# Second block's layer norms: the mean is spread a second time, kept in SBUF, and GpSimd subtracts it from the last chunks

## The chip, the cores and the metric

The kernel runs on one core of one Trainium2 chip. The metric is the device time of the whole program in microseconds. A time per run and, for one profiled execution, a hardware trace are at hand. TensorE is called PE (its weight loads PEld), VectorE DVE, ScalarE ACT, GpSimd POOL, and SyncE SP.

## The reference

Two transformer-like blocks run one after the other on one sequence of 512 tokens and 1024 features, all in float32. The first block is an SSM and sliding-window attention mixer followed by a gated FFN, with RMS norms. The second block has two layers, called "a" (dilated attention) and "h" (HGRN2). Each layer has two deep-norm residual steps:

```
x = layer_norm(ALPHA * x + mixer(x), ln_mix_g[i], ln_mix_b[i])
x = layer_norm(ALPHA * x + squared_relu_mlp(x), ln_ffn_g[i], ln_ffn_b[i])

def layer_norm(x, g, b):
    mu = mean(x, axis=-1);  var = mean(square(x - mu), axis=-1)
    return (x - mu) * rsqrt(var + 1e-5) * g + b
```

So the second block has four layer norms: `mix_a`, `ffn_a`, `mix_h`, `ffn_h`. The text calls them the first, second, third and fourth norm. They lie at about 1265, 1627, 1886 and 2250 us of the trace. The result of the fourth is the output of the kernel.

## The kernel before

Activations are held feature-major: a tensor of 1024 features by 512 tokens is eight chunks (`DC` = 8), each 128 partitions (features) by 512 columns (tokens). Every dense product is done in three matmuls of rounded parts: `w_lo*x_hi`, `w_hi*x_lo`, `w_hi*x_hi`. ACT makes the rounded high part (`w_hi`, `x_hi`) with a copy that rounds; DVE makes the low part as the difference (`w_lo = raw - w_hi`, `x_lo = h - x_hi`), with both inputs in SBUF. Weights come in slabs of 128 x 2048 by SP's DMA queue into two slots.

Each engine has its own program with explicit semaphores; the order within an engine is the order written. `settle` is DVE's drain.

How a layer norm goes. PE sums the chunks over features token by token with matmuls of one column (`token_sum`, L687). DVE makes the mean by token (`mean4`, 128 x 4, L2450) and the variance (L2455), ACT its root (L1601), DVE the reciprocal (`rstd4`, L2459). PE spreads both over 128 partitions with four transposes each (`spread`, L694): the mean into PSUM bank 4 (`SPREAD_MEAN`), then the reciprocal root into bank 5. Then DVE goes through the chunks (`layer_norm`, L2461 on): it subtracts the mean from chunks 0 and 1 (L2462), and for each chunk c multiplies by the reciprocal root (L2466, "mul c" in the text) and then subtracts the mean from chunk c+2 (L2468, "sub c+2"). Both instructions read one operand from SBUF (`y`) and one from PSUM.

In the first three norms more work of DVE lies in the same loop, because the next stage of matmuls starts on the chunks as they are finished. For chunks 0 and 1 DVE also makes `h` (gain and bias, a TENSOR_SCALAR from SBUF to SBUF, L2471) and `x_lo` (L1731). After `x_lo` of chunk 1 it makes the low part of the second weight slab (`second_lo`, L1717, two halves; one half before `hgrn_in`, in the second norm). From chunk 2 on, ACT makes `h` (L1609) and then `x_hi` (L1611) of each chunk, and DVE makes `x_lo` of chunk c-1 after mul c. In the fourth norm (`after` is `None`) ACT makes `h` of every chunk, and SP sends it out.

PE's next stage is `first_pair` (first and third norm, L617, L622, L627) or `first_triple` (second norm, L1219, L1224, L1229). It goes by a written order of (weight slab, chunk) steps; for `first_pair` it is `(0,0), (0,1), (1,0), (1,1), (0,2), (0,3), (0,4), (1,2), ...`, each step six matmuls. A step waits for `x_hi` of its chunk before its first two matmuls and for `x_lo` before its last two; step (1,0) waits for `w_lo` of the second slab before its middle two. For `first_triple` the order is `(0,0), (0,1), (1,0), (0,2), ...`, and a step of slab 1 has three matmuls.

POOL is used in the first block for `accumulate` (L522 and L525, two-operand instructions on 128 x 512 chunks in SBUF) and then only to issue small DMAs in the attention (`send`, the last at 1183 us). In the four layer norms it does nothing.

The buffer `root` (128 x 512, SBUF) holds the shift used in the variance sums of the norm (ACT writes it, L1593; DVE reads it, L2394, L2396, L2422); it is free while the loop of L2461 on runs. PSUM bank 6 (`MEAN`) holds the sums by token until DVE has read them at L2450.

Of the kernel before, what the change touches and what calls it, by code (L numbers as in the profile page):

```python
# [18 lines left out]
DC = D // P  # L19
# [76 lines left out]
def build(nc, w, x_in, gains_in, lam_in, sink_in, bc_in, c_in, pos_in, iota_in, const_in, freq_in, mask_in, rope2_in,  # L96
          hmask_in, out):
    f32, f32r, bf16, i32 = mybir.dt.float32, mybir.dt.float32r, mybir.dt.bfloat16, mybir.dt.int32
    ALU, ACT, AX = mybir.AluOpType, mybir.ActivationFunctionType, mybir.AxisListType
# [33 lines left out]
    y = at("y", Y_AT, [DC, T])  # L133
# [76 lines left out]
    root = extra("root", [T])  # L210
# [49 lines left out]
    ps = nc.alloc_psum_tensor("ps", [P, 8, T], f32)  # L260
# [44 lines left out]
    def sem(name):  # L305
        return nc.alloc_semaphore(name)
# [20 lines left out]
    folded = sem("folded")  # L327
    var4_ready = sem("var4_ready")
    mean_ready = sem("mean_ready")
    root_ready = sem("root_ready")  # L330
    result_ready = sem("result_ready")
    rstd_ready = sem("rstd_ready")
# [79 lines left out]
    LO_SPLITS1 = {1: 0, 6: 1, 8: 2, 13: 3}  # L412
    GLUS1 = {8: 1, 11: 2, 14: 3}
    NEAR2 = [min(b, 1) + 1 for b in range(TB)]

    def shift_at(st):

# [51 lines left out]
    with nc.Block() as block:  # L469
# [40 lines left out]
        @block.gpsimd  # L510
        def _(pool):
            for pads in (ab_re, ab_neg, ca_re, ca_im):
                last = pool.memset(pads[:, :, :, :], 0.0)
            last.then_inc(pads_zero, 1)
            pool.wait_ge(mask_ready, 1)
            pool.memset(k_tau[:, :, :, :], 0.0).then_inc(kt_zero, 1)

            def accumulate(name, event):

                for c in range(DC - 1):  # L520
                    pool.wait_ge(y_ready, YB[event] + c + 1)
                    last = pool.tensor_tensor(acc_sq if c else acc, y[:, c, :], y[:, c, :], ALU.mult)  # L522
                    if c:
                        pool.drain()
                        last = pool.tensor_tensor(acc, acc, acc_sq, ALU.add)  # L525
                    if c < DC - 2:
                        pool.drain()
                last.then_inc(acc_ready, 1)

            def send(pa, old):  # L530

                pool.wait_ge(o2_ready, TB * pa + TB)
                if not (isinstance(pa, int) and pa == 0):
                    pool.wait_ge(joined, pa)
                pool.sem_inc(sums_sent, 1)
                for hh in range(2):
                    for b in range(TB):
                        pool.dma_start(o_far[:, hh, b, :], o_class[32 * b:32 * b + 32, old, hh, :, :]).then_inc(far_ready, 16)

            for name, event in ACCS[:2]:  # L540
                accumulate(name, event)
            send(0, 0)
            with pool.Fori(0, HEAD_PAIRS // 2 - 1) as i:
                send(2 * i + 1, 1)
                send(2 * i + 2, 0)

        @block.tensor
        def _(pe):
# [148 lines left out]
            def spread_rstd(name):  # L697
                pe.wait_ge(rstd_ready, SK_ROOT[name] + 1)
                spread(SPREAD[name], rstd4).then_inc(rstd_spread, 1)
# [365 lines left out]
            def dense_normed(name, part, layer, xs=None, hid=None, operand=None, begun=0):  # L1065
# [42 lines left out]
                pe.wait_ge(mean4_ready, nth + 1)  # L1108
                spread(SPREAD_MEAN, mean4).then_inc(mean_spread, 1)
                spread_rstd(var)  # L1110

            def norm_and_ffn(layer, proj, up, down):

# [135 lines left out]
        def _(act):  # L1249
# [352 lines left out]

            def normed(layer, part, n, after):

                for c in range(DC):
                    act.wait_ge(y_ready, YB[f"res_{part}_{layer}"] + c + 1)
                    g, b = gain(f"ln_{part}_g{n}", c), gain(f"ln_{part}_b{n}", c)
                    if c > 1 or not after:
                        last = act.activation(h[:, c, :], y[:, c, :], ACT.Identity, scale=g, bias=b)  # L1609
                    if after:  # L1610
                        act.activation(x_hi[:, c, :], y[:, c, :], ACT.Identity, scale=g, bias=b).then_inc(xhi_ready, 1)  # L1611
                    else:
                        last.then_inc(result_ready, 1)

            def norm_and_ffn(layer, proj, up, down, n, after):
                normed_out(proj, layer, "mix")
# [82 lines left out]
        def _(dve):  # L1699
# [746 lines left out]
            def layer_norm(layer, part, n, after):  # L2446
# [16 lines left out]
                settle()  # L2463
                dve.wait_ge(rstd_spread, NTH_SPREAD[var] + 1)
                for c in range(DC):
                    tt(y[:, c, :], y[:, c, :], scale, ALU.mult).then_inc(y_ready, 1)  # L2466
                    if c + 2 < DC:
                        tt(y[:, c + 2, :], y[:, c + 2, :], mean, ALU.subtract)  # L2468
                    if after and c < 2:
                        settle()  # L2470
                        ts(h[:, c, :], y[:, c, :], gain(f"ln_{part}_g{n}", c), gain(f"ln_{part}_b{n}", c), ALU.mult, ALU.add)  # L2471
                        settle()
                        part_lo(after, c, h[:, c, :])
                        if c:
                            for half in range(1 if after == "hgrn_in" else 2):
                                second_lo("hgrn_in" if after == "hgrn_in" else after + "0", half)
                    elif after and c > 2:
                        part_lo(after, c - 1, h[:, c - 1, :])
                    if c + 2 < DC:
                        settle()  # L2480
# [244 lines left out]
```

## Time and profile before

| what | value |
|---|---|
| time before, median of 3 runs | 2270.08 us |
| lowest and highest | 2269.61 and 2271.3 us |
| span of the profiled execution (first to last instruction) | 2267.5 us |
| own time of the profiled execution | not recorded; 2.6 us more than its span if it was a median run |
| PE busy | 2165.4 us (95% of the span) |
| DVE busy | 1271.7 us (56%) |
| ACT busy | 885.9 us (39%) |
| POOL busy | 84.4 us (4%) |
| mean granted TensorE clock | 0.970 |

The page has one execution: the busy time by engine, the span in 40 slices, the DMA queues, the chain of work that ended last, and groups of instructions. Positions below are microseconds from the start of the span. A timeline row has the start, the duration, the engine, the line and the tiles, and in brackets the idle time of the engine before it and what ended it. "PE 1.12 x4" is a merged row of four instructions: the time is from the start of the first to the end of the last. Durations of neighbours on an engine overlap by about 0.1 us.

### The profile page before, as it was taken

How to read it: one execution, taken by the hardware profiler on the slowest of the kernel's cores; microseconds unless marked ns; L12 is line 12 of the kernel's file. 1: busy time of each engine (PE TensorE's matmuls, PEld its weight loads, DVE VectorE, ACT ScalarE, POOL GpSimd, SP SyncE). 2: the span in 40 equal slices, each digit the busy share in tenths (PEclk: the TensorE clock that was granted, in tenths of full speed). 3: DMA queues.
4: the chain of work that ended last, by engine and by line, in shares of the span. 5: the costliest groups of instructions: out<-in, count | busy, mean ns of one | idle time of the engine just before them, and what ended most of it. 6: DMA issues, size and time to landing. Idle time of an engine off the chain costs nothing.

```text
span 2267.5 us, 29414 instructions
## 1 busy us (share of the span) xinstructions
PE 2165.4 (95%) x11002; PEld 1771.0 (78%) x11002; DVE 1271.7 (56%) x2003; ACT 885.9 (39%) x1298; POOL 84.4 (4%) x91
## 2 busy tenths in 40 slices
PE   6979899999999999999999899999999998999997
PEld 5747778888877888888877688888777776888886
DVE  6986464434455566665566742344568877423444
ACT  4224233222227555565553431242254534312322
POOL 1000300000130000000000000000000000000000
PEclk9989999999999999999989899999999998999998
DMA  4001322233232212222221132222212121322221
GB/s 166 30 10 56 112 75 92 84 103 107 73 116 84 89 49 87 72 86 70 84 83 56 56 101 103 93 93 93 75 56 74 56 93 56 104 101 93 93 93 56
DMA packets 32980, 185.48 MB, mean 82 GB/s; under 512 B 5760, under 2 KB 6144, under 8 KB 14208
## 3 DMA queue, kind: packets, MB, share of 16 engines
q1 hardware_dynamic: 27792, 176.31, 22.6%
q10 hardware_dynamic: 3312, 6.14, 0.8%
q0 software_dynamic: 1792, 1.90, 0.3%
q8 instruction: 55, 0.90, 0.2%
q14 instruction: 29, 0.24, 0.0%
HBM read 180.06 MB, written 2.10 MB: 80 GB/s over the span
## 4 chain that ended last, share of the span: by engine, by line
PE 81%; DVE 10%; DVEq 4%; ACT 2%; issue 1%; DMA 1%; ACTq 0%
PE ps L566 12%; PE ps L567 12%; PE ps L568 12%; PE ps L1047 5%; PE ps L1049 5%; PE ps L1048 5%; PE ps L1098 2%; PE ps L1100 2%; PE ps L1099 2%; PE ps L687 1%; PE ps L627 1%; PE ps L617 1%; PE ps L984 1%; PE ps L967 1%; PE ps L980 1%
## 5 line engine op out<-in xcount | busy, mean ns | idle before, releaser
L1268 ACT ACTIVATE w_hi<-raw 128x2048 fp32r<-128x2048 f32 (+1 forms) x122 | 226.1, 1853 | 298.6 <-PE ps L568 220.2
L566 PE MATMUL ps<-x_hi,w_lo 128*128 128x512 f32 x816 | 317.6, 389 | 0.5 <-DVE y L2185 0.3
L568 PE MATMUL ps<-x_hi,w_hi 128*128 128x512 f32 x816 | 317.5, 389 | 0.0
L567 PE MATMUL ps<-x_lo,w_hi 128*128 128x512 f32 x816 | 317.4, 389 | 0.0
L1708 DVE TENSOR_TENSOR w_lo<-raw,w_hi 128x2048 fp32r<-128x2048 f32 (+3 forms) x116 | 259.2, 2235 | 93.9 <-ACT w_hi L1268 93.6
L1047 PE MATMUL ps<-x_hi,w_lo 128*128 128x512 f32 x544 | 218.9, 402 | 2.4 <-DVE w_lo L2337 2.4
L1049 PE MATMUL ps<-x_hi,w_hi 128*128 128x512 f32 x544 | 213.2, 392 | 0.0
L1048 PE MATMUL ps<-x_lo,w_hi 128*128 128x512 f32 x544 | 212.3, 390 | 0.0
L566 PEld LDWEIGHTS ps<-x_hi,w_lo 128*128 128x128 f32 x816 | 153.2, 188 | 33.0 <-issue 0.7
L568 PEld LDWEIGHTS ps<-x_hi,w_hi 128*128 128x128 f32 x816 | 153.2, 188 | 31.9
L567 PEld LDWEIGHTS ps<-x_lo,w_hi 128*128 128x128 f32 x816 | 153.2, 188 | 31.6
L568 PE MATMUL ps<-hid_hi,w_hi 128*128 128x512 f32 x378 | 147.1, 389 | 0.0
L566 PE MATMUL ps<-hid_hi,w_lo 128*128 128x512 f32 x378 | 147.0, 389 | 0.0
L567 PE MATMUL ps<-hid_lo,w_hi 128*128 128x512 f32 x378 | 147.0, 389 | 0.0
L2337 DVE TENSOR_TENSOR w_lo<-raw,w_hi 128x2048 fp32r<-128x2048 f32 x38 | 87.1, 2291 | 76.1 <-ACT w_hi L1481 75.8
L2369 DVE TENSOR_TENSOR tmp<-tmp 128x512 f32<-128x512 f32 x64 | 44.2, 691 | 144.7 <-ACT hid_hi L1560 144.6
L1049 PEld LDWEIGHTS ps<-x_hi,w_hi 128*128 128x128 f32 x544 | 102.5, 188 | 22.6
L1047 PEld LDWEIGHTS ps<-x_hi,w_lo 128*128 128x128 f32 x544 | 102.6, 189 | 21.8 <-DVE w_lo L2337 2.8
L1048 PEld LDWEIGHTS ps<-x_lo,w_hi 128*128 128x128 f32 x544 | 102.9, 189 | 19.7
L1518 ACT ACTIVATE swapped<-ps 32x512 f32<-32x512 f32 x192 | 113.0, 589 | 2.3
L1558 ACT ACTIVATE tmp<-ps 128x512 f32<-128x512 f32 x64 | 38.2, 597 | 178.2 <-PE ps L568 175.3
L1509 ACT ACTIVATE qkv<-ps 128x512 f32<-128x512 f32 x72 | 42.9, 597 | 142.2 <-PE ps L1049 141.9
(452 smaller groups left out, 4050.3 us busy)
## 6 DMA issues: line engine op xcount, KB each, us to landing
raw<-w_attn_in SPq DMA_DIRECT2D x32, 1024.0 KB, 4.9
raw<-w_gate_up SPq DMA_DIRECT2D x22, 1024.0 KB, 4.9
raw<-w_up_a SPq DMA_DIRECT2D x16, 1024.0 KB, 4.8
raw<-w_down_a SPq DMA_DIRECT2D x16, 1024.0 KB, 4.9
raw<-w_up_h SPq DMA_DIRECT2D x16, 1024.0 KB, 4.9
raw<-w_down_h SPq DMA_DIRECT2D x16, 1024.0 KB, 4.9
raw<-w_hgrn_in SPq DMA_DIRECT2D x8, 1024.0 KB, 4.8
raw<-w_down SPq DMA_DIRECT2D x8, 768.0 KB, 4.3
```

The source lines that it names most:

```text
L566: pe.matmul(o, w_lo[:, slot, a:a + P], hi[:, k, :], start=k == 0, stop=False)
L567: pe.matmul(o, w_hi[:, slot, a:a + P], lo[:, k, :], start=False, stop=False)
L568: last = pe.matmul(o, w_hi[:, slot, a:a + P], hi[:, k, :], start=False, stop=k == st.kc - 1)
L1047: pe.matmul(o, w_lo[:, slot, a:a + P], x_hi[:, k, :], start=k == 0, stop=False)
L1048: pe.matmul(o, w_hi[:, slot, a:a + P], x_lo[:, k, :], start=False, stop=False)
L1049: last = pe.matmul(o, w_hi[:, slot, a:a + P], x_hi[:, k, :], start=False, stop=k == DC - 1)
L1098: pe.matmul(o, w_lo[:, slot, a:a + P], hi[:, k, :], start=k == 0, stop=False, skip_group_check=True)
L1099: pe.matmul(o, w_hi[:, slot, a:a + P], lo[:, k, :], start=False, stop=False, skip_group_check=True)
L1268: act.activation(w_hi[:, slot, 0:width], raw[:, slot, 0:width], ACT.Copy).then_inc(whi_ready, 1)
L1518: last = act.activation(turned[to:to + 32], bank[at_:at_ + 32], ACT.Copy)
L1708: tt(w_lo[:, slot, 0:width], raw[:, slot, 0:width], w_hi[:, slot, 0:width].bitcast(f32), ALU.subtract) \
L2337: tt(w_lo[:, n0 % 2, :], raw[:, n0 % 2, :], w_hi[:, n0 % 2, :].bitcast(f32), ALU.subtract) \
```

## The change

- PE: after the reciprocal root is spread, the mean is spread once more, into bank 6 (`MEAN`), and signalled by `mean_again`.
- ACT: `keep_mean` waits for that and copies bank 6 to `root` in SBUF, signalled by `mean_kept`. In the first three norms the copy stands after `x_hi` of chunk 0; in the fourth it stands before the first chunk.
- POOL: at the end of its program it waits in each norm for `mean_kept` and subtracts `root` from chunks 4 to 7 (in the fourth norm 5 to 7) of `y` in place, each signalled by `centred`.
- DVE: it leaves out L2468 for these chunks and waits for `centred` before it multiplies them.

```diff
--- before.py
+++ after.py
@@ -327,6 +327,7 @@
     folded = sem("folded")
     var4_ready = sem("var4_ready")
     mean_ready = sem("mean_ready")
+    mean_again, mean_kept, centred = sem("mean_again"), sem("mean_kept"), sem("centred")
     root_ready = sem("root_ready")
     result_ready = sem("result_ready")
     rstd_ready = sem("rstd_ready")
@@ -412,6 +413,8 @@
     LO_SPLITS1 = {1: 0, 6: 1, 8: 2, 13: 3}
     GLUS1 = {8: 1, 11: 2, 14: 3}
     NEAR2 = [min(b, 1) + 1 for b in range(TB)]
+    ON_POOL = [(4, 5, 6, 7)] * 3 + [(5, 6, 7)]
+    CENTRED = [0, 4, 8, 12]
 
     def shift_at(st):
 
@@ -543,6 +546,10 @@
             with pool.Fori(0, HEAD_PAIRS // 2 - 1) as i:
                 send(2 * i + 1, 1)
                 send(2 * i + 2, 0)
+            for nth in range(len(MEANS)):
+                pool.wait_ge(mean_kept, nth + 1)
+                for c in ON_POOL[nth]:
+                    pool.tensor_tensor(y[:, c, :], y[:, c, :], root[:, :], ALU.subtract).then_inc(centred, 1)
 
         @block.tensor
         def _(pe):
@@ -1108,6 +1115,7 @@
                 pe.wait_ge(mean4_ready, nth + 1)
                 spread(SPREAD_MEAN, mean4).then_inc(mean_spread, 1)
                 spread_rstd(var)
+                spread(MEAN, mean4).then_inc(mean_again, 1)
 
             def norm_and_ffn(layer, proj, up, down):
 
@@ -1602,6 +1610,14 @@
 
             def normed(layer, part, n, after):
 
+                nth = MEANS[f"mean_{part}_{layer}"]
+
+                def keep_mean():
+                    act.wait_ge(mean_again, nth + 1)
+                    act.activation(root[:, :], ps[:, MEAN, :], ACT.Copy).then_inc(mean_kept, 1)
+
+                if not after:
+                    keep_mean()
                 for c in range(DC):
                     act.wait_ge(y_ready, YB[f"res_{part}_{layer}"] + c + 1)
                     g, b = gain(f"ln_{part}_g{n}", c), gain(f"ln_{part}_b{n}", c)
@@ -1611,6 +1627,8 @@
                         act.activation(x_hi[:, c, :], y[:, c, :], ACT.Identity, scale=g, bias=b).then_inc(xhi_ready, 1)
                     else:
                         last.then_inc(result_ready, 1)
+                    if after and c == 0:
+                        keep_mean()
 
             def norm_and_ffn(layer, proj, up, down, n, after):
                 normed_out(proj, layer, "mix")
@@ -2463,8 +2481,10 @@
                 settle()
                 dve.wait_ge(rstd_spread, NTH_SPREAD[var] + 1)
                 for c in range(DC):
+                    if c in ON_POOL[nth]:
+                        dve.wait_ge(centred, CENTRED[nth] + c + 1 - ON_POOL[nth][0])
                     tt(y[:, c, :], y[:, c, :], scale, ALU.mult).then_inc(y_ready, 1)
-                    if c + 2 < DC:
+                    if c + 2 < DC and c + 2 not in ON_POOL[nth]:
                         tt(y[:, c + 2, :], y[:, c + 2, :], mean, ALU.subtract)
                     if after and c < 2:
                         settle()
```

## Rows read from the trace of the kernel before

**Rows 1.** The page: the span, and the chain that ended last by engine.
```profile
span 2267.5 us, 29414 instructions
...
PE 81%; DVE 10%; DVEq 4%; ACT 2%; issue 1%; DMA 1%; ACTq 0%
```

**Rows 2.** Chain, first norm: start us, us, engine, written tile, line.
```profile
1277.28 0.69 DVE y L2466
...
1284.54 0.73 PE ps L627 x2
```

**Rows 3.** Timeline, first norm: start us, us, instruction, [idle before <-releaser].
```profile
1268.28 1.12 PE L694 MATMUL ps<-consts,by_token 128*128 128x128 f32 x4 [0.98 <-DVE by_token L2459]
...
1270.19 0.81 ACT L1611 ACTIVATE x_hi<-y,gains 128x512 fp32r<-128x512 f32 x1 [1.06 <-DVE y L2466]
...
1271.45 0.69 DVE L1731 TENSOR_TENSOR x_lo<-h,x_hi 128x512 fp32r<-128x512 f32 x1
...
1273.60 0.55 DVE L2471 TENSOR_SCALAR h<-y,gains 128x512 f32<-128x512 f32 x1
...
1274.22 0.69 DVE L1731 TENSOR_TENSOR x_lo<-h,x_hi 128x512 fp32r<-128x512 f32 x1
...
1274.83 2.35 DVE L1717 TENSOR_TENSOR w_lo<-raw,w_hi 128x1024 fp32r<-128x1024 f32 x2
...
1277.24 0.74 PE L622 MATMUL ps<-x_hi,w_lo 128*128 128x512 f32 x2 [1.07 <-DVE w_lo L1717]
...
1277.88 0.68 DVE L2468 TENSOR_TENSOR y<-y,ps 128x512 f32<-128x512 f32 x1
...
1282.56 0.73 PE L627 MATMUL ps<-x_lo,w_hi 128*128 128x512 f32 x2 [0.32 <-DVE x_lo L1731]
```

**Rows 4.** Chain, second norm, columns as in rows 2.
```profile
1638.46 0.70 DVE y L2466
...
1640.00 0.71 ACT x_hi L1611
...
1640.75 0.73 PE ps L1219 x2
```

**Rows 5.** Timeline, fourth norm, columns as in rows 3.
```profile
2257.35 0.69 DVE L2466 TENSOR_TENSOR y<-y,ps 128x512 f32<-128x512 f32 x1
...
2262.80 1.28 DVE L2466 TENSOR_TENSOR y<-y,ps 128x512 f32<-128x512 f32 x2
2263.52 1.52 ACT L1609 ACTIVATE h<-y,gains 128x512 f32<-128x512 f32 x2 [0.55 <-DVE y L2466]
```

**Rows 6.** Line L1593: duration ns min/median/max, first and last start us.
```profile
L1593 ACT ACTIVATE root<-ps x4: 598/599/599, 1236.1 to 2174.6; 128x512 f32<-128x512 f32 x4
```

**Rows 7.** Timeline of POOL and DVE in the first block, columns as in rows 3.
```profile
252.70 1.29 POOL L525 TENSOR_TENSOR tmp<-tmp 128x512 f32<-128x512 f32 x1
...
614.50 1.04 POOL L522 TENSOR_TENSOR tmp<-y 128x512 f32<-128x512 f32 x1 [5.77 <-DVEq L2191]
614.89 1.99 DVE L1708 TENSOR_TENSOR w_lo<-raw,w_hi 128x1280 fp32r<-128x1280 f32 x1 [0.52 <-ACT w_hi L1268]
615.68 2.35 POOL L525 TENSOR_TENSOR tmp<-tmp 128x512 f32<-128x512 f32 x1
```

**Rows 8.** Lines L1708 (603 to 650 us) and L2549, columns as in rows 6.
```profile
L1708 DVE TENSOR_TENSOR w_lo<-raw,w_hi x8: 1493/2152/2294, 603.7 to 649.5; 128x1280 fp32r<-128x1280 f32 x4, 128x2048 fp32r<-128x2048 f32 x4
...
L2549 DVE TENSOR_SCALAR state<-state,f_cum x48: 285/286/290, 1675.9 to 1841.2; 128x128 f32<-128x128 f32 x48
L2549 DVE TENSOR_SCALAR state<-ps,f_cum x8: 351/352/353, 1675.1 to 1836.4; 128x128 f32<-128x128 f32 x8
```

**Rows 9.** Windows, first norm: busy us of each engine, granted clock, DMA share.
```profile
1256.00:1257.00 1.00, 0.00 (x0) 0.00 (x0) 0.93 (x3) 0.04 (x1) 0.00 (x0) 1.00 0.00 0
1257.00:1258.00 1.00, 0.28 (x2) 0.31 (x2) 0.52 (x1) 0.00 (x0) 0.00 (x0) 0.64 0.00 0
...
1274.00:1275.00 1.00, 1.00 (x5) 0.74 (x5) 0.93 (x3) 0.00 (x0) 0.00 (x0) 0.83 0.00 0
```

## The prediction

> **What bounds the kernel now.** I read the page first: its chain goes through PE for 81% of the span and through DVE for 10% [rows 1]. In the middle of a matmul stage an instruction taken from DVE is worth nothing; around the layer norms PE stands still or waits for chunks, and there DVE is the chain. So I went through the chain and the timeline around the four norms.
>
> First norm: DVE starts mul 2 at 1277.28, and that is on the chain; the last time PE is behind DVE is the last pair of step (0,4), at 1284.54, which ends at 1285.27 [rows 2]. From there PE is the chain. Before that, PE waits 1.07 us for `w_lo` of the second slab and then only fractions such as 0.32 us for `x_lo` [rows 3]. So what the end of the norm pays for has two halves. The stretch up to mul 2 (DVE makes `h`, `x_lo` of chunks 0 and 1, and `w_lo`) is paid in full. Behind it, the loop over chunks 2 to 4 is paid only as far as PE catches up with it. The third norm has the same rows. In the second, mul 2 at 1638.46 goes through ACT's `x_hi` to PE at 1640.75, and behind this PE is the chain [rows 4]: there, all of the cost of DVE up to mul 2 counts, and nothing after it. In the fourth norm there is no PE work left; DVE's loop and ACT's last `h` are the end of the program [rows 5].
>
> **What the change removes.** It takes four L2468 from the first three norms each, three from the fourth. One is 0.68 us [rows 3], 0.60 from start to start, and all of them stand behind mul 2.
>
> Fourth norm: mul 2 to mul 6 take 2262.80 - 2257.35 = 5.45 us for four chunks, 1.36 each [rows 5]. Mul 3 stays at 2258.71. Without sub 5 to 7 a mul follows the last after 0.69 + 0.07 = 0.76: mul 6 starts at 2261.0 and ends at 2261.7 instead of 2263.5. ACT's last two `h` hang on it as before, 0.71 apart [rows 5]. The output DMA follows each `h`. Gain 1.8 us, all at the end of the program. It needs POOL in time: I put the end of the spread near 2254.9 (mul 0 starts at 2254.63), the copy takes 0.60 [rows 6], so POOL starts at about 2255.6; at 1.29 us for a two-operand instruction of this shape [rows 7] it has finished chunks 5, 6, 7 by 2259.5, and DVE wants them at 2260.2 to 2261.6. All of DVE's instructions here have `y` in SBUF and the other operand in PSUM.
>
> First norm, were POOL free of charge: mul 2 stays, mul 3 to 7 come closer. But ACT makes two instructions per chunk, 0.71 us apart, so chunks can't come faster than 1.42 us, where they come every 1284.54 - 1282.56 = 1.98 now [rows 2, 3] (mul, sub, `x_lo` and a drain). `x_hi` of chunk 2 is then ready at 1277.28 + 0.69 + 0.02 + 0.71 + 0.81 = 1279.5 as now, that of chunk 4 at 1282.5. Step (0,4) of PE, six matmuls in 1.38 us, ends at 1284.2 instead of 1285.27: gain 1.0. Third norm the same, second norm nothing, because PE takes no time from DVE behind mul 2. With the fourth norm: -3.8 us. That is the most the change can give.
>
> **What it adds.** PE: four more transposes, 1.12 us as a row of four at the lower clock [rows 3], while PE would stand idle until `x_hi` of chunk 0; nothing. ACT: one copy, 599 ns [rows 6], after `x_hi` of chunk 0, where ACT has over a microsecond free until mul 1; nothing (0.1 us in the fourth norm, under mul 1). Behind ACT's wait for the spread stand `h` and `x_hi` of later chunks, none due yet. The queues of SP are not touched; POOL has nothing behind its waits.
>
> POOL and DVE together are the disputed cost. In the first block POOL did L525 in 1.29 us when DVE was idle, and in 2.35 us when DVE had begun a `w_lo` before it: it ended 1.15 us after DVE. The other way round, L522 runs from 614.50 to 615.54 and the DVE's L1708 that starts at 614.89 takes 1.99 us [rows 7] where the quickest of this shape takes 1.49 [rows 8]: 0.50 us of waiting, 0.15 less than the overlap. So an instruction of DVE with both operands in SBUF and a two-operand one of POOL do not run together; the later one waits for the whole of the earlier. The page "SBUF — State Buffer" of the Trainium skill, section "Who interferes with whom", says so: DVE with two SBUF inputs and GpSimd reading SBUF exclude one another for a whole instruction. By that rule, the trace agrees.
>
> Does L2471, one operand, SBUF to SBUF, also exclude POOL? L2549 takes 286 ns from SBUF and 352 from PSUM on 128 columns [rows 8], 66 ns less, and 0.55 us on 512 columns against 0.69 for others [rows 3]: the SBUF form is the quicker one, so it may use a second way to SBUF. I take it that it waits. "VectorE: DVE Perf Modes", section "The perf-mode tier table", gives a float32 `tensor_scalar` in SBUF the double rate, with both read ports; by that it would stand in POOL's way too. If it did not, the delay would be some 0.6 us less in each of three norms, and the sum below 4.0 instead of 5.8.
>
> Where does POOL's work fall? First norm: ACT's copy starts at 1270.19 + 0.72 = 1270.9, ends at 1271.5, POOL starts at 1271.6. DVE's `x_lo` of chunk 0 has begun at 1271.45 [rows 3], so sub 4 runs from about 1272.1 to 1273.3 and sub 5 to 1274.5. These are the very microseconds in which DVE has `h` (1273.60), `x_lo` (1274.22) and two halves of `w_lo` (1274.83 to 1277.18), all SBUF [rows 3]. If both take turns, `h` waits 0.9 us for sub 5, `x_lo` 1.2 for sub 6, the first half of `w_lo` 1.2 for sub 7, less three times the 0.15: 2.9 us late at mul 2. If POOL goes through without giving way, `h` waits 3.3: nearly the same. Bounds: below 0 to 0.3 (DVE never gives way and POOL fits in behind), above 3.3. I take 2.9, by the exclusion seen both ways in rows 7.
>
> First norm with 2.9: mul 2 at 1280.2, `x_hi` of chunk 4 at 1285.4 (by ACT's 1.42 and once more DVE), step (0,4) ends at 1286.9: +1.6. Third +1.6. Second norm: the same three waits (one half of `w_lo` only), +2.9 in full. Fourth -1.8. Together +4.3.
>
> The clock: PE is idle through the window at 1256 and most of that at 1257, and within the latter its granted clock falls from 1.00, that is from 2.4 to 1.2 GHz (mean 0.64); it comes back in the window at 1274, where PE has worked for some microseconds [rows 9]. Now PE is to idle 1.07 + 2.9 = 4.0 us before `w_lo` [rows 3], as long as there or longer. If the clock falls for some 3 us of work, these cost 1.5 us more, less what PE waits anyway. Between 0 and 1.4 us for each of three norms; I take 0.5 each, +1.5. Sum +5.8: 2267.5 + 5.8 = 2273.3 of span; the median of the runs shown is 2.6 us above the span, so **2276 us**.
>
> **Rivals.** (A) DVE keeps SBUF through instructions that stand without a drain between them (`x_lo`, both `w_lo`): POOL gets in only at the two drains. Delay 0.75 + 1.05 = 1.8: first and third norm +0.6, second +1.8, fourth -1.8, sum +1.2, and up to 2.5 of clock: 2271 to 2274, say 2272.5. For it: DVE's neighbours overlap. Against: nothing in the rows shows an engine that is passed over when it waits. (B) The other sign: POOL costs DVE next to nothing, at most 0.3 us per norm, because the waiting POOL always loses to DVE's next instruction, or because the long rows of L525 have another cause. It holds if the delay stays under 1.4 us per norm; then -3.5: 2266.5. For it: DVE does not need chunk 4 before about 1280, so POOL may come last without harm. Against it: the 0.50 us that L1708 waited. (C) The delay, and the clock falls in every norm for long, or POOL is slow to begin after its long rest: +4.3 + 4.2 or more, 2279 and above. (D) The delay is absorbed further on, by slack in the next stage: 2270. Against it: PE is the chain there [rows 1].
>
> **Numbers.** Mine 0.42, A 0.22, B 0.25, C 0.07, D 0.04. The measurement can tell about 0.2%, 4.5 us, from no change. Faster by that would need more than the 3.8 us above: 0.04. Mine lies over it nine times in ten (0.38), A seldom (0.06), C always: slower 0.51. Same 0.45. The range reaches from B to the lower end of C: 2266 to 2280; for my case alone 2273 to 2279.5.
>
> **What would show it.** L2471 and L1731 of chunk 1 and L1717 with rows over 1.3 us in the first three norms; L2468 nine times instead of 24; POOL rows of 1.3 to 2.5 us beside them; mul 2 of the first three norms 2 to 3.3 us later after mul 0 than now; PE's clock lower in the stretch behind `w_lo`; the last `h` 1.8 us sooner after mul 0 of the fourth norm. I am wrong if DVE's rows keep their lengths (B), if only one or two of them grow (A), or if POOL's first instruction starts late enough to miss this stretch.

## The result, and the profile after

The changed kernel takes 2275.88 us (median of 8 runs, 2272.62 to 2278.81), the kernel before on the same chip 2270.02 us (8 runs, 2268.45 to 2271.3). The ratio is 1.0027, 95% interval 1.0018 to 1.0037: 5.9 us slower, and the interval excludes 1. In the later runs of the same kernel (`e9` below) it was 1.0024 (1.0014 to 1.0034). The profiled execution has its own time, 2276.1 us, and a span of 2274.3 us, 6.8 more than the span before. In every run whose span is on record the time is 1.7 to 1.9 us above the span, so the profiled execution before took about 2269.3 us, 0.7 less than its median; that is most of the difference between 6.8 and 5.9.

The page of the changed kernel: span, busy time by engine, and the chain by engine.

```profile
span 2274.3 us, 29450 instructions
...
PE 2164.5 (95%) x11018; PEld 1768.4 (78%) x11018; DVE 1271.7 (56%) x1988; ACT 888.1 (39%) x1302; POOL 106.4 (5%) x106
...
PE 83%; DVE 9%; DVEq 4%; ACT 2%; issue 1%; DMA 1%; ACTq 0%
```

DVE's busy time is 1271.7 us, as before, although it has 15 subtractions fewer. Those took 0.60 us each from start to start, 9.0 together; 8.0 of it is back in the three rows per norm that follow. DVE's timeline of the changed kernel in the first norm, from mul 0 to mul 2 (L2486 is mul, L2488 sub, L2491 `h`, L1749 `x_lo`, L1735 `second_lo`):

```profile
1271.36 0.69 DVE L2486 TENSOR_TENSOR y<-y,ps 128x512 f32<-128x512 f32 x1
...
1272.72 0.55 DVE L2491 TENSOR_SCALAR h<-y,gains 128x512 f32<-128x512 f32 x1
1273.34 0.69 DVE L1749 TENSOR_TENSOR x_lo<-h,x_hi 128x512 fp32r<-128x512 f32 x1
1274.13 0.69 DVE L2486 TENSOR_TENSOR y<-y,ps 128x512 f32<-128x512 f32 x1
...
1275.49 1.20 DVE L2491 TENSOR_SCALAR h<-y,gains 128x512 f32<-128x512 f32 x1
1276.77 1.61 DVE L1749 TENSOR_TENSOR x_lo<-h,x_hi 128x512 fp32r<-128x512 f32 x1
1278.30 3.44 DVE L1735 TENSOR_TENSOR w_lo<-raw,w_hi 128x1024 fp32r<-128x1024 f32 x2
1281.83 1.47 DVE L2486 TENSOR_TENSOR y<-y,ps 128x512 f32<-128x512 f32 x2
```

And what POOL does, its timeline in the four norms (one merged row each; in brackets how long it had idled and for what):

```profile
1273.46 6.06 POOL L552 TENSOR_TENSOR y<-y,root 128x512 f32<-128x512 f32 x4 [88.78 <-ACT root L1617]
...
1637.09 6.05 POOL L552 TENSOR_TENSOR y<-y,root 128x512 f32<-128x512 f32 x4 [357.56 <-ACT root L1617]
1901.68 6.05 POOL L552 TENSOR_TENSOR y<-y,root 128x512 f32<-128x512 f32 x4 [258.55 <-ACT root L1617]
2263.78 3.73 POOL L552 TENSOR_TENSOR y<-y,root 128x512 f32<-128x512 f32 x3 [356.05 <-ACT root L1617]
```

The fourth norm shows what one subtraction takes when nothing with both operands in SBUF runs beside it: 3.73 / 3 = 1.24 us. In the first three, four take 6.06, 1.1 us more than 4 x 1.24; one by one their records in the first norm are 1.71, 1.28, 1.46 and 1.73 us long. The same microseconds, 1273.5 to 1279.5, hold DVE's `h`, `x_lo` and first half of `w_lo`, which grew by 0.65, 0.92 and 1.09 us over rows 3 (0.55, 0.69, 2.35). That is 2.66 us, and mul 2 comes 2.7 us later. In DVE's work for chunk 0, before POOL begins, every row is as it was.

How PE pays for it. The chain of the changed kernel in the first norm: start, us, engine, written tile, line.

```profile
1275.49 1.20 DVE h L2491
...
1276.77 1.61 DVE x_lo L1749
1278.38 2.23 DVEq L2500
1280.61 1.15 DVE w_lo L1735
...
1281.80 0.73 PE ps L629 x2
...
1287.19 0.73 PE ps L624 x2
...
1288.39 0.46 PE ps L634 x2
```

The kernel before has mul 0 of this norm here:

```profile
1269.47 0.69 DVE L2466 TENSOR_TENSOR y<-y,ps 128x512 f32<-128x512 f32 x1
```

The lengthened rows are themselves links. PE waits until 1281.80 for `w_lo` of the second slab, and step (0,4) ends at 1288.85, 17.49 us after mul 0, where it was 1285.27 - 1269.47 = 15.80.

In the fourth norm all goes the other way. DVE and ACT of the changed kernel, timeline:

```profile
2267.27 3.62 DVE L2486 TENSOR_TENSOR y<-y,ps 128x512 f32<-128x512 f32 x5
2267.99 3.86 ACT L1625 ACTIVATE h<-y,gains 128x512 f32<-128x512 f32 x5 [0.55 <-DVE y L2486]
```

Five muls now follow one another at 0.73 us, and the last `h` ends 8.67 us after mul 0 (2263.18), where rows 5 give 2265.04 - 2254.63 = 10.41.

The following table is worked out from such rows of both timelines, each stretch from the start of mul 0 of its norm. "PE's end" is the end of step (0,4) in the first and third norm and of the 72 matmuls of `first_triple` in the second.

| stretch | before | after | difference |
|---|---|---|---|
| mul 1 to mul 2, first / second / third | 5.04 / 3.91 / 5.04 | 7.70 / 6.55 / 7.70 | +2.66 / +2.64 / +2.66 |
| mul 0 to PE's end, first | 15.80 | 17.49 | +1.69 |
| mul 0 to PE's end, second | 22.32 | 27.44 | +5.12 |
| mul 0 to PE's end, third | 15.80 | 17.47 | +1.67 |
| mul 0 to the last `h`, fourth | 10.41 | 8.67 | -1.74 |

For the second norm, mul 0 and the last matmul of the 72, before (the first two rows) and after:

```profile
1631.78 0.69 DVE L2466 TENSOR_TENSOR y<-y,ps 128x512 f32<-128x512 f32 x1
1653.71 0.39 PE L1229 MATMUL ps<-x_lo,w_hi 128*128 128x512 f32 x1
...
1634.99 0.69 DVE L2486 TENSOR_TENSOR y<-y,ps 128x512 f32<-128x512 f32 x1
1662.04 0.39 PE L1237 MATMUL ps<-x_lo,w_hi 128*128 128x512 f32 x1
```

It has 2.5 us above its wait of 2.64. Windows of the changed kernel there: us of the window, then busy us of PE, PEld, DVE, ACT and POOL, granted clock, DMA share, GB/s.

```profile
1641.00:1642.00 1.00, 0.00 (x0) 0.00 (x0) 1.00 (x2) 0.00 (x0) 1.00 (x2) 0.98 0.00 0
1642.00:1643.00 1.00, 0.93 (x2) 0.83 (x3) 1.00 (x2) 0.00 (x0) 1.00 (x1) 0.50 0.00 0
...
1651.00:1652.00 1.00, 1.00 (x4) 0.77 (x3) 1.00 (x3) 0.88 (x3) 0.00 (x0) 0.50 0.00 0
1652.00:1653.00 1.00, 1.00 (x6) 0.82 (x5) 0.65 (x2) 1.00 (x2) 0.00 (x0) 0.90 0.00 0
```

PE stands still in the window at 1641, waiting for `x_lo`, and from 1642 its granted clock is 0.50 (1.2 GHz) until about 1652, with PE busy for most of it: 4 matmuls in the window at 1651, 6 in the next. In the kernel before the clock was low in this norm too, but from 1629 to 1639.5, when PE mostly waited for DVE anyway.

### The profile page after: what moved, and what is told of

Same layout as the page of the kernel before. It is cut to its first block, busy times and chain, and to the rows that moved or that the text cites. A ratio compares the mean times of both kernels' runs of the same rounds, so it can differ in the third digit from the quotient of the medians.

```text
span 2274.3 us, 29450 instructions
## 1 busy us (share of the span) xinstructions
PE 2164.5 (95%) x11018; PEld 1768.4 (78%) x11018; DVE 1271.7 (56%) x1988; ACT 888.1 (39%) x1302; POOL 106.4 (5%) x106
## 4 chain that ended last, share of the span: by engine, by line
PE 83%; DVE 9%; DVEq 4%; ACT 2%; issue 1%; DMA 1%; ACTq 0%
PE ps L573 12%; PE ps L575 12%; PE ps L574 12%; PE ps L1054 5%; PE ps L1056 5%; PE ps L1055 5%; PE ps L1105 2%; PE ps L1106 2%; PE ps L1107 2%; PE ps L624 1%; PE ps L629 1%; PE ps L634 1%; PE ps L991 1%; PE ps L603 1%; PE ps L974 1%
```

## The experiments

All are edits of the changed kernel, each timed beside the kernel before on the same chip. `e1` to `e4` ran together (before: 2269.37 us), `e5` to `e8` together (before: 2270.11), `e9` and `e10` together (before: 2269.43). Each ratio is to the kernel before. The diffs show the lines that matter; `CENTRED` is worked out from `ON_POOL` in all that change it. In `e8` and `e10` the 11 added matmuls lie within the stretch to PE's end. Their stretches:

| kernel | median us | ratio (95%) | mul 1 to mul 2 | PE's end, 1st / 2nd / 3rd | last `h`, 4th |
|---|---|---|---|---|---|
| e1 fourth norm only | 2267.41 | 0.9994 (0.9985 to 1.0003) | 5.04 / 3.90 / 5.04 | 15.80 / 22.29 / 15.81 | 8.66 |
| e2 first three only | 2276.08 | 1.0035 (1.0023 to 1.0048) | 7.70 / 6.55 / 7.70 | 17.50 / 27.47 / 17.49 | 10.40 |
| e3 POOL only writes | 2267.01 | 0.9989 (0.9980 to 0.9998) | 5.04 / 4.71 / 5.83 | 14.84 / 24.56 / 15.62 | as e1 |
| e4 POOL later | 2268.53 | 0.9996 (0.9987 to 1.0005) | 5.04 / 3.90 / 5.04 | 15.95 / 24.51 / 15.91 | as e1 |
| e5 chunks 6, 7 | 2269.77 | 0.9999 (0.9990 to 1.0008) | 5.71 / 4.58 / 5.70 | 15.75 / 22.96 / 15.76 | as e1 |
| e6 fourth norm, four chunks | 2267.38 | 0.9989 (0.9980 to 0.9998) | as before | as before | 8.07 |
| e7 spread and copy only | 2268.98 | 0.9998 (0.9989 to 1.0007) | as before | 15.80 / 22.30 / 15.80 | 10.40 |
| e8 filler in the second norm | 2278.42 | 1.0034 (1.0022 to 1.0046) | as after | 18.72 / 24.87 / 19.01 | as after |
| e9 the changed kernel again | 2274.60 | 1.0024 (1.0014 to 1.0034) | 7.71 / 6.57 / 7.70 | 18.70 / 26.62 / 17.48 | as after |
| e10 filler again | 2276.71 | 1.0031 (1.0022 to 1.0040) | as after | 19.98 / 24.9 / 18.73 | as after |

**The two halves.** `e1` leaves the subtractions of the first three norms to DVE, `e2` those of the fourth; the second spread and the copy stay in all four.

```diff
-    ON_POOL = [(4, 5, 6, 7)] * 3 + [(5, 6, 7)]
+    ON_POOL = [(), (), (), (5, 6, 7)]
```

and for `e2`

```diff
-    ON_POOL = [(4, 5, 6, 7)] * 3 + [(5, 6, 7)]
+    ON_POOL = [(4, 5, 6, 7)] * 3 + [()]
```

> POOL subtracts in the fourth norm only (chunks 5 to 7); the second spread and the copy to SBUF stay in all four. Theory T (DVE's instructions with SBUF operands and POOL's take turns; this is all of the loss): the first three norms are as in the kernel before, h and x_lo of chunk 1 at 0.55 and 0.69 us, mul 1 to mul 2 at 5.04, 3.91 and 5.04 us; the fourth norm 1.7 us shorter; time 2270.0 - 1.7 = 2268.3 us. Rival R (the loss comes from the added spread and copy, or from the clock that they disturb): these stay, so the time remains at about 2275 us.

> The other half: POOL subtracts in the first three norms and not in the fourth. Theory T: first and third norm +1.7 us each, second +2.6 us and about 1 us of clock, nothing gained at the end: 2270.0 + 7 = 2277 to 2278 us. Rival R: as the changed kernel plus the lost end gain, 2277.6 us as well, so this run does not tell them apart but shows if the parts add up: e1 and e2 together should differ from before by as much as the changed kernel, +5.9 us.

`e1` is 2.0 us below the kernel before, `e2` 6.7 above it; together +4.8, against +5.9 and +5.2 for the whole. The stretches say it more sharply than the medians: in `e1` the first three norms are to 0.03 us those of before and the fourth has its 8.66; in `e2` it is the other way round. So there are two separate effects, with opposite signs; the interval of `e1` by itself includes 1, that of `e2` doesn't.

**The additions alone.** `e7` keeps the spread and the copy in all four norms and gives POOL nothing.

```diff
+    ON_POOL = [(), (), (), ()]
```

> The additions alone: the second spread and the copy to SBUF in all four norms, POOL subtracts nothing and DVE does as before. Theory T: no cost, 2270 us, first three norms as before, fourth within 0.1 us. Rival R: some of the loss of the changed kernel, 2271 us or more, or a clock that falls or comes back at other places than before.

Every stretch is that of before to 0.02 us. The copy of the first norm lies where the prediction put it, behind `x_hi` of chunk 0, with ACT idle for a while after it. ACT's timeline of `e7`:

```profile
1270.69 0.81 ACT L1627 ACTIVATE x_hi<-y,gains 128x512 fp32r<-128x512 f32 x1 [1.06 <-DVE y L2486]
1271.41 0.57 ACT L1617 ACTIVATE root<-ps 128x512 f32<-128x512 f32 x1
...
1273.47 0.81 ACT L1627 ACTIVATE x_hi<-y,gains 128x512 fp32r<-128x512 f32 x1 [1.48 <-DVE y L2486]
```

PE's four transposes and ACT's copy cost nothing; all of the loss is POOL's instructions.

**Is it the reading?** `e3` puts in place of POOL's subtractions in the first three norms instructions that read nothing, one for each. They write zeros to a scratch tile, with a drain of POOL behind each, so this kernel leaves out the mean of chunks 4 to 7 in those norms; it is of use for its times alone.

```diff
                 for c in ON_POOL[nth]:
-                    pool.tensor_tensor(y[:, c, :], y[:, c, :], root[:, :], ALU.subtract).then_inc(centred, 1)
+                    if nth < 3:
+                        pool.memset(tmp[:, 0:2, :], 0.0).then_inc(centred, 1)
+                        pool.drain()
+                    else:
+                        pool.tensor_tensor(y[:, c, :], y[:, c, :], root[:, :], ALU.subtract).then_inc(centred, 1)
```

> In the first three norms POOL does not subtract but writes zeros into a scratch buffer (128 x 1024, four times, about 0.9 us each) at the same moment, so the mean is missing from chunks 4 to 7 there; the fourth norm is as in the changed kernel. Theory T, with the page that says only a GpSimd instruction that reads SBUF stands in the way of a two-operand one of DVE: x_lo of chunk 1 and both w_lo keep 0.69 and 1.22 us; h of chunk 1 may wait for one write. First and third norm then gain 1.0 us each less at most 0.7: time 2266.5 to 2269 us. Rival W (POOL at work slows DVE whatever it does): rows of DVE grow as in the changed kernel, 2274 us or more.

DVE's timeline of `e3` in the second norm, from `h` of chunk 1 on:

```profile
1635.74 1.35 DVE L2495 TENSOR_SCALAR h<-y,gains 128x512 f32<-128x512 f32 x1
1637.16 0.69 DVE L1753 TENSOR_TENSOR x_lo<-h,x_hi 128x512 fp32r<-128x512 f32 x1
1637.77 1.22 DVE L1739 TENSOR_TENSOR w_lo<-raw,w_hi 128x1024 fp32r<-128x1024 f32 x1
```

POOL works beside them, from 1633.68 to 1637.97; its last write covers the whole of `x_lo` and the first 0.2 us of `w_lo`. Both keep the lengths of before: two operands in SBUF do not mind a POOL that only writes, which `x_lo` shows for its whole length and `w_lo` for a short overlap. `h` does mind: 1.35 us instead of 0.55 (1.34 in the third norm). So the two kinds of DVE instruction meet POOL in different ways, the two-operand one over the reading, the one-operand SBUF-to-SBUF one also over the writing. The record of the third write starts 0.1 us behind that of `h`, and `h` ends 0.3 us after it, so the records do not tell by their starts which instruction has SBUF first.

The Trainium skill says in "SBUF — State Buffer", section "Who interferes with whom", that DVE with two SBUF inputs contends with a GpSimd instruction that reads, "not with one that only writes it". The trace agrees (`x_lo` 0.69 us). The same section says that DVE in a two-port mode, which `tensor_scalar` can enter, contends with GpSimd, and makes no such exception for writes. The 1.35 us of `h` agree with that; that `h` runs in such a mode is inferred from its 0.55 us against the 0.69 of the others, and no row names the mode.

In the first norm `h` was spared, since POOL did no work then. POOL's timeline of `e3`:

```profile
1272.70 0.95 POOL L553 MEMSET tmp<- 128x1024 f32 x1 [88.71 <-ACT root L1621]
1278.39 3.14 POOL L553 MEMSET tmp<- 128x1024 f32 x3 [4.74 <-issue]
...
1633.68 4.29 POOL L553 MEMSET tmp<- 128x1024 f32 x4 [352.16 <-ACT root L1621]
```

The second write begins 4.74 us after the first one's end, and the row names no wait. What lies between is the drain that the edit added (L554): its record lasts 5.64 us and ends at 1278.32, 4.67 after the write, while the eight of the second and third norm last 1.02 to 1.11 us each, write included. It is not peculiar to this kernel. The first drain of POOL behind its small DMAs of the attention ends 4.66 us after the last of them in the kernel before, and 4.67 us after POOL's last work at the end of `e1`, `e4`, `e5`, `e6` and of the changed kernel. In `e7`, where POOL has done nothing for over a millisecond when it comes, it lasts 4.65 us, in `e2`, behind twelve subtractions and 350 us of rest, 4.65 as well; in `e3`, which has paid for it in the first norm, the drain at the end takes 0.06. Why the first drain takes so long no run shows. It makes this norm the one where POOL is nearly free of charge: PE's end is at 14.84, a gain of 0.96. The prediction gave a free POOL 1.0. In the second norm PE's end is 2.2 us late for a wait of 0.8; there the granted clock is 0.50 from about 1641 to 1645 in this execution.

**Another time for the same work.** `e4` lets POOL begin only when DVE has passed `w_lo` and done mul 2.

```diff
             for nth in range(len(MEANS)):
                 pool.wait_ge(mean_kept, nth + 1)
+                if nth < 3:
+                    pool.wait_ge(y_ready, YB["res_" + ("mix_a", "ffn_a", "mix_h")[nth]] + 3)
```

> In the first three norms POOL waits for mul 2 before its first subtraction, so that h and x_lo of chunk 1 and w_lo are over when it begins. Theory T: mul 1 to mul 2 back at 5.04, 3.91 and 5.04 us; the turns now fall on x_lo of chunks 2 to 5, each up to 0.9 us late, where the next chunk comes 1.4 us later, so the gain of 1.0 us in the first and third norm is mostly eaten, and the second pays 0 to 1 us: together 0 to +1.5 us, with the fourth norm's 1.7 us a time of 2268.3 to 2269.8 us. Rival R: the start of POOL does not matter, about 2276 us.

Mul 1 to mul 2 is back at its old length. POOL now meets the three `x_lo` of the loop. DVE's timeline of `e4`, first norm:

```profile
1278.44 1.67 DVE L1751 TENSOR_TENSOR x_lo<-h,x_hi 128x512 fp32r<-128x512 f32 x1 [0.81 <-ACT x_hi L1629]
...
1280.81 1.00 DVE L1751 TENSOR_TENSOR x_lo<-h,x_hi 128x512 fp32r<-128x512 f32 x1
...
1282.51 1.01 DVE L1751 TENSOR_TENSOR x_lo<-h,x_hi 128x512 fp32r<-128x512 f32 x1
```

POOL's timeline of `e4`, the same stretch:

```profile
1277.00 5.96 POOL L554 TENSOR_TENSOR y<-y,root 128x512 f32<-128x512 f32 x4 [96.12 <-DVE y L2488]
```

These waits sum to 0.98 + 0.31 + 0.32 = 1.6 us, yet PE's end moves by 0.15 and 0.10 only: DVE no longer subtracts here, so the loop has the time to give. With the same work of POOL the first norm ends 1.69 us later in one place and 0.15 in another. In the second norm the end is 2.2 us late although all waits ahead of mul 2 are gone; there the granted clock is 0.50 from about 1642 to 1645 in this execution, which accounts for some 1.6 us (3.2 us of work at half speed), and PE waits 0.46 us at 1641.63 for the lengthened `x_lo` of chunk 2, a wait that the kernel before doesn't have. Counted from mul 0 of the second norm to mul 0 of the third, `e4` is 0.65 us over the kernel before.

**Fewer instructions of POOL.** `e5` leaves it chunks 6 and 7.

```diff
+    ON_POOL = [(6, 7)] * 3 + [(5, 6, 7)]
```

> In the first three norms POOL subtracts two chunks (6 and 7) in place of four; the fourth norm as in the changed kernel. Theory T (turns): only h of chunk 1 meets POOL, at its second instruction; mul 1 to mul 2 is 0.65 us longer than before in each of the three norms (5.69, 4.56, 5.69 us), and x_lo of chunk 1 and both w_lo keep 0.69 and 1.22 us. First and third norm: 0.65 later at mul 2, up to 1.1 caught up by step (0,4): -0.4 each; second +0.65 and 0 to 2.5 of clock; fourth -1.7: 2267.5 to 2270 us. Rival P (the loss is a fixed cost of POOL reading SBUF beside DVE, not one per meeting): mul 1 to mul 2 near 7.7, 6.5 and 7.7 us as in the changed kernel, about 2274 us.

DVE's timeline of `e5`, first norm:

```profile
1275.65 1.21 DVE L2491 TENSOR_SCALAR h<-y,gains 128x512 f32<-128x512 f32 x1
1276.94 0.69 DVE L1749 TENSOR_TENSOR x_lo<-h,x_hi 128x512 fp32r<-128x512 f32 x1
1277.55 2.35 DVE L1735 TENSOR_TENSOR w_lo<-raw,w_hi 128x1024 fp32r<-128x1024 f32 x2
```

POOL's timeline of `e5`, the same stretch:

```profile
1273.63 2.96 POOL L552 TENSOR_TENSOR y<-y,root 128x512 f32<-128x512 f32 x2 [87.57 <-ACT root L1617]
```

With two subtractions only the first meeting is left, and it costs what it did (0.66). One meeting goes with one instruction of POOL: the third and fourth are what `x_lo` and `w_lo` wait for in the changed kernel. That is the turn-taking order of the forecast. The median is that of the kernel before.

**The version that the halves point to.** `e6` has spread, copy and POOL in the fourth norm alone, and gives POOL chunk 4 as well.

```diff
-    ON_POOL = [(4, 5, 6, 7)] * 3 + [(5, 6, 7)]
+    ON_POOL = [(), (), (), (4, 5, 6, 7)]
...
-                spread(MEAN, mean4).then_inc(mean_again, 1)
+                if ON_POOL[nth]:
+                    spread(MEAN, mean4).then_inc(mean_again, 1)
```

> The version that the first runs point to: spread, copy and POOL in the fourth norm only, there with four chunks (4 to 7) on POOL. POOL starts 1.2 us after mul 0 starts less a little, needs 1.24 us per chunk, so chunk 4 is there at mul 0 + 2.0, chunk 7 at mul 0 + 5.7; DVE wants them at mul 0 + 4.3 to + 6.4. Mul 3 follows mul 2 after 0.75 in place of 1.36 us: the last h ends 0.6 us sooner than with three chunks, 2.35 us sooner than before. Theory T: 2270.0 - 2.35 = 2267.6 us. Rival (the output DMA takes over, since six chunks now come every 0.76 us): no more than the 1.7 us of three chunks, 2268.3 us.

Timeline of `e6`, fourth norm (mul 0 starts at 2253.69):

```profile
2254.86 4.93 POOL L552 TENSOR_TENSOR y<-y,root 128x512 f32<-128x512 f32 x4 [1073.88 <-ACT root L1618]
...
2256.41 4.40 DVE L2485 TENSOR_TENSOR y<-y,ps 128x512 f32<-128x512 f32 x6
2257.13 4.63 ACT L1626 ACTIVATE h<-y,gains 128x512 f32<-128x512 f32 x6 [0.54 <-DVE y L2485]
```

POOL is just in time: it ends at 2259.79, and mul 7 starts at about 2260.1 (five muls of 0.73 behind mul 2), so no mul waits. The last `h` ends 8.07 us after mul 0, 2.34 sooner than in the kernel before and 0.59 sooner than in `e1`.

Little of these 0.59 us reaches the end of the program. From mul 0 to the end of the span it is 12.85 us in the kernel before (2267.5 - 2254.63), 11.1 in `e1` and 11.0 in `e6`. The last output has landed at 2263.82, but the drain at the end of POOL's program is not over yet: line L472 of `e6`, duration ns min/median/max, first and last start us.

```profile
L472 POOLq DRAIN  x1: 9643/9643/9643, 2254.8 to 2254.8; - x1
```

It ends at about 2264.5, 4.7 us after POOL's last subtraction, and the span at 2264.7. In `e1` the same drain ends at 2263.61, ahead of the last output (2264.78). So the fourth chunk brought 0.1 us, and what limited it is that first drain of POOL, neither DVE nor the output DMA that the expectation named as the rival. A drain of POOL earlier, where nothing waits for it, was not tried. The median is 2267.38, 2.7 us below that of before on the same chip, ratio 0.9989 (0.9980 to 0.9998): faster than both kernels, if by little. Against `e1` (2267.41, with the kernel before at 2269.37) no gain is shown.

**The clock.** `e8` puts 11 matmuls into a PSUM bank that nothing reads at that time, where PE waits in the second norm (5, 2 and 4 of them), to keep PE at work there.

```diff
+                def fill(n):
+                    for _ in range(n):
+                        pe.matmul(ps[:, SUM, :], w_hi[:, st.slab0 % 2, 0:P], x_hi[:, 0, :], start=True, stop=True,
+                                  skip_group_check=True)
...
+                    if (c, k) == (0, 2):
+                        fill(4)
...
+                    if (c, k) == (1, 0):
+                        fill(2)
...
+                        if (c, k) == (0, 1):
+                            fill(5)
```

> The changed kernel, with eleven added matmuls in the second norm's first_triple (into a PSUM bank that nothing reads then), in the gaps in which PE waits: five before the x_lo of chunk 1, two before w_lo, four before x_hi of chunk 2. Theory T with clock: the second norm's extra 5.1 us are 2.6 us of DVE's turns and 2.5 us of PE at the lower clock after its long idle stretch; kept at work, PE stays at the full clock, mul 0 to the end of the 72 matmuls falls from 27.4 to about 25 us, and the time is 2273.4 us where the changed kernel has 2275.9. Rival (the 2.5 us are waits of PE for chunks and not the clock): nothing gained, 2276 us or a little more.

In its own norm it did what it was made for. Windows of `e8`, columns as above:

```profile
1642.00:1643.00 1.00, 1.00 (x6) 0.56 (x4) 1.00 (x2) 0.00 (x0) 1.00 (x2) 1.00 0.00 0
...
1912.00:1913.00 1.00, 1.00 (x4) 0.78 (x3) 0.54 (x1) 1.00 (x2) 0.00 (x0) 0.50 0.86 352
```

The clock is at 1.00 where it was 0.50, and PE's end in the second norm is at 24.87 instead of 27.44: 2.57 us back, so the excess above the wait was the clock. But the total did not fall. The second row shows the third norm of the same execution, 12 us behind its mul 0, still at 0.50.

To see whether that is a property of the program or of the execution, the changed kernel and this one ran once more, side by side.

> The changed kernel once more, without an edit, to be laid beside the next run on the same chip. If the waits of DVE set its time, the median is 2276 within 1 us and mul 1 to mul 2 takes 7.70, 6.55 and 7.70 us again, to 0.05 us. If the phase in which TensorE's clock falls is drawn anew in each execution, the stretches of low granted clock lie elsewhere than in the first profile of this kernel (1263 to 1276, 1642 to 1652, 1891 to 1904); if they hang on the program alone, they lie within 2 us of the same places, and mul 0 of the second norm to the end of step 72 matmuls takes 27.4 us again.

> The kernel with 11 filler matmuls in the second norm once more. Its first profile had 11.5 us of TensorE work lost to the low clock in the third norm where the changed kernel had 5.6 (busy time times the missing share of the clock, window by window), and 7.3 against 5.6 in the first. If these losses are drawn anew in each execution, this profile shows other ones and the median comes out within 1 us of that of the changed kernel in this call, less up to 2.5 us for the clock in the second norm: 2273.5 to 2277. If the fillers move the fall of the clock in the third norm by their own place in the program, that norm again loses over 9 us and the median is 2277 to 2279.

Windows of `e9`, the changed kernel in another execution:

```profile
1641.00:1642.00 1.00, 0.95 (x3) 0.49 (x3) 1.00 (x1) 0.00 (x0) 1.00 (x1) 1.00 0.00 0
...
1643.00:1644.00 1.00, 0.72 (x2) 0.50 (x2) 0.91 (x2) 0.00 (x0) 0.00 (x0) 0.50 0.00 0
...
1648.00:1649.00 1.00, 1.00 (x4) 0.81 (x3) 0.83 (x2) 1.00 (x2) 0.00 (x0) 0.50 0.00 0
```

The next table goes through the windows of 1 us around the first three norms (1240 to 1310, 1610 to 1680, 1865 to 1935) and sums the busy time of PE times the missing share of its clock: the PE time that full clock would have saved, whether or not PE was the bound.

| execution | span | first | second | third | low clock in the third |
|---|---|---|---|---|---|
| before | 2267.5 | 5.3 | 6.5 | 6.9 | 1882 to 1898 |
| after | 2274.3 | 5.6 | 7.1 | 5.6 | 1891 to 1904 |
| e9, the same kernel | 2271.3 | 7.2 | 7.7 | 4.1 | 1888 to 1891, 1895 to 1901 |
| e8, filler | 2276.6 | 7.3 | 4.5 | 11.5 | 1887 to 1914 |
| e10, the same kernel | 2278.2 | 11.7 | 4.5 | 9.0 | 1889 to 1906, 1913 to 1916 |

Between the two executions of the changed kernel the waits of DVE agree to 0.03 us, and the stretches of low clock do not agree: in the first norm it ends at 1276 in one and returns from 1281 to 1284 in the other, which puts PE's end there at 18.70 instead of 17.49. The page "TensorE: Matmul & The Clock Gate" of the Trainium skill, section "Part 1: The HAM clock gate", says that the gate looks at activity by a rhythm of its own, so the same kernel shows another number of slow matmuls each time; by that rule, these two executions agree. The second norm of the filler kernel is 4.5 both times, against 7.1 and 7.7: that gain repeats, and so does PE's end, 24.87 and 24.9. Its losses in the first and third norms are larger than those of the changed kernel both times, 18.8 and 20.7 together against 11.2 and 11.3. The medians are 2278.42 and 2276.71, against 2275.88 and 2274.60: not faster, and its interval overlaps that of the changed kernel. The two profiles are not typical of their kernels: the profiled execution of `e9` is 1.5 us below its median, that of `e10` 3.3 us above. The first norm lies ahead of the filler, so what it loses there in both executions can't come from added matmuls that have not run yet; it may be chance. Whether the filler makes the third norm lose more stays open.

## Why the prediction was right, step by step

Forecast 2276, measured 2275.88; span +5.8 forecast, +6.8 measured in the profiled execution. The waits alone make +4.26 in the ledger above (1.69 + 2.64 + 1.67 - 1.74); the forecast had +4.3 for them.

The whole span can be laid out from mul 0 to mul 0. Against the kernel before, the first profile of the changed kernel has +1.9 us before mul 0 of the first norm, then +1.3, +3.7 and +1.65 up to mul 0 of the second, third and fourth, and -1.7 from there to the end: +6.8. The second profile (`e9`) has -0.3, +2.5, +1.8, +1.65 and -1.7: +3.9. The part behind mul 0 of the first norm is +4.9 in one and +4.2 in the other; since the waits agree, the difference is put down to the clock. That the forecast of 2276 met the median to 0.1 us is luck in the clock's term: the same kernel is 5.9 us over the kernel before in one set of runs and 5.2 in the other.

- **The waits of DVE**, 2.9 us in each of three norms: measured 2.66, 2.64, 2.66 (`h` 0.65, `x_lo` 0.92, `w_lo` 1.09 or 1.07; forecast 0.75, 1.05, 1.05 after its deduction). Right in kind, in order and in place. The size is a little high; 0.05 of each meeting is POOL's subtraction, which took 1.24 us and not the 1.29 of rows 7. `e5` shows that the meetings are with single instructions of POOL, `e7` that nothing else in the change costs anything.
- **That `h` stands in POOL's way**: right, 0.65 us of the 2.66, and `e3` shows that even a POOL that only writes delays it. The reason given for it, a second way to SBUF, is inferred from lengths. That row was expected over 1.3 us and has 1.20; `x_lo` and `w_lo` are above that mark.
- **First and third norm**, +1.6 each: measured +1.69 and +1.67 where the clock did not interfere. PE catches up behind mul 2 as it was worked out.
- **Second norm**, the wait paid in full: the clock-free figure is 24.87 (`e8`), 2.55 above the 22.32 of before, forecast 2.9.
- **Fourth norm**, -1.8: measured -1.74, and in `e1` 10.41 - 8.66 = 1.75.
- **The additions** at nothing: `e7` agrees to 0.02 us.
- **The clock**, +0.5 for each norm: the sum was near and the split was not. In the first profile it was 0 in the first norm, 2.5 in the second, 0 in the third; in the second profile of the same kernel 1.2, 1.7 and 0 (18.70 - 17.49, 26.62 - 24.87). It is not a share for each norm but a draw in each execution: the waits open a second idle stretch in a place where PE is about to be the bound, and the fall of the clock may or may not hit it. The first norm also began 1.9 us later than before, ahead of anything the change touches. That is scatter from far earlier: the matmul of PE that starts at 1250.19 in the kernel before starts 2.67 us later in this execution, and in `e9` 0.33 earlier.

The rivals. A, that DVE keeps SBUF through neighbours without a drain, falls on one row: there is no drain between `x_lo` of chunk 1 and `w_lo`, and `w_lo` waited 1.09 us all the same. B, that POOL costs next to nothing, falls on all three rows; what B would have given is seen in the first norm of `e3` (-0.96, by 1.0 in the forecast). C, the clock falling for long in every norm, was not so in either profile; nor was POOL slow to begin (ACT's copy in the first norm ends at 1272.81 + 0.57 = 1273.38, POOL starts at 1273.46). D, absorption later on, falls on the total.

What stays open is the difference between the parts and the whole (+4.8 from `e1` and `e2`, +5.9 and +5.2 measured), which is within what the clock scatters, and the behaviour of the filler.

## What to carry to other kernels

Before work is moved from DVE to POOL, look at what DVE has in those same microseconds: moving SBUF-to-PSUM instructions away gains only what their engine had on the path, while an SBUF-to-SBUF instruction of DVE that meets a two-operand one of POOL waited here for half to nine tenths of it (0.65 to 1.09 of 1.24 us). In the first and third norm the same four subtractions cost 1.7 us beside `h`, `x_lo` and `w_lo` and about 0.1 a few microseconds later (`e4`). Three of them gained 1.7 us in the norm in which all of DVE's instructions have an operand in PSUM. A fourth brought the last `h` 0.6 us forward there and the end of the program 0.1, so look at the end of every engine's program too.

A wait in a stretch where PE is the bound can cost more than its length when the clock falls in it (5.12 us for a wait of 2.64 in the second norm), and how much more differs from one execution to the next; so judge such a change by stretches counted from a common event, and by the median only after several runs.

## What the runs showed of the hardware that was not expected

- Turns are taken even between instructions of DVE that otherwise overlap: a waiting POOL got SBUF between `x_lo` and `w_lo`, and DVE got it back after one subtraction (`x_lo` 1.61 us for 0.69, the first half of `w_lo` 2.3 for 1.22).
- A POOL instruction that only writes 128x1024 float32 (0.95 us, 4.29 for four with their drains) delays a one-operand SBUF-to-SBUF instruction of DVE by 0.80 us and two-operand ones not at all (`e3`).
- The low stretches of TensorE's clock are from about 3 to 27 us long around these norms, and their place shifts from one execution of a kernel to the next, while the stretch from mul 1 to mul 2 repeats to 0.05 us. Two executions of the changed kernel had spans 3.0 us apart.
- The first drain of POOL behind its small DMAs takes 4.65 us or a little more beyond POOL's last work, even if it comes over a millisecond after them (`e7`); later ones took less than 0.1 (`e3`). In `e6` it is the end of the program.
